# Neighbourhood attention in one fp32 encoder-layer kernel: prompt tiles of 8 columns by 16 rows with three key blocks

## What is computed

```python
r0 = jnp.clip(r - kh // 2, 0, rows - kh)      # kh = 8 (4 in the sample)
c0 = jnp.clip(c - kw // 2, 0, GRID_W - kw)    # kw = 16
bias = rpb[:, dr + (NA_KH - 1), dc + (NA_KW - 1)]
s = einsum('bqhd,bqnhd->bhqn', q_r, k_r) * scale + bias
out = einsum('bhqn,bqnhd->bqhd', softmax(s), v_r)
```

## Time and profile before

| | |
|---|---|
| median of 3 runs | 2660.97 us (2659.28 to 2661.75) |
| the profiled execution | 2659.89 us |
| its span in the trace | 2658.1 us |
| PE busy | 2525.8 us (95%) |
| DVE, ACT, POOL busy | 1561.6 us (59%), 1276.1 us (48%), 392.6 us (15%) |
| chain that ended last, by engine | PE 94%, DVE 3%, ACT 1%, issue 1% |
| of it on lines of attention | L1463 3%, L1476 2%, and part of L1325's 28% |
| granted PE clock, mean | 0.966 |

### The profile page before, as it was taken

The page is one execution under the profiler, slowest core; times in us unless marked ns, Lnnn a source line. Parts: engine busy times, 40 slices in busy tenths (PEclk is TensorE's granted clock), DMA queues, the critical chain, the costliest instruction groups (busy, mean ns, idle before and its releaser), DMA issues.

```text
span 2658.1 us, 43740 instructions
## 1 busy us (share of the span) xinstructions
PE 2525.8 (95%) x17770; PEld 2144.8 (81%) x17770; DVE 1561.6 (59%) x2106; ACT 1276.1 (48%) x1826; POOL 392.6 (15%) x221
## 2 busy tenths in 40 slices
PE   7979999999999989829999999999999999999997
PEld 4666767767777668629999999999999999999997
DVE  3343242341010133368888888887888888888885
ACT  3113243331000021217767776776677667767763
POOL 0041201011111100020220221022012202210210
PEclk9988999999999999959999999999999999999999
DMA  8111101010010133328988988898899889888972
GB/s 185 35 32 30 30 8 30 0 40 24 24 47 24 32 151 133 142 83 284 296 270 291 312 285 267 300 317 270 288 304 296 271 282 322 285 276 303 321 269 84
DMA packets 338366, 481.41 MB, mean 181 GB/s; under 512 B 22059, under 2 KB 194746, under 8 KB 338209
## 3 DMA queue, kind: packets, MB, share of 16 engines
q1 hardware_dynamic: 331072, 454.26, 50.9%
q0 software_dynamic: 7136, 24.93, 4.7%
HBM read 454.29 MB, written 24.87 MB: 180 GB/s over the span
## 4 chain that ended last, share of the span: by engine, by line
PE 94%; DVE 3%; issue 1%; ACT 1%; DMA 0%; POOL 0%; SPq 0%; DVEq 0%; ACTq 0%; POOLq 0%
PE ps L1615 35%; PE ps L1325 28%; PE ps L1618 16%; PE ps L1538 4%; PE ps L1463 3%; PE ps L1476 2%; PE ps L1605 1%; PE ps L1606 1%; PE ps L1423 1%; PE ps L1654 1%; PE ps L1655 1%; DVE top_i L1208 0%; DVE aff L1210 0%; DVE top_v L1207 0%; PE ps L1548 0%
## 5 line engine op out<-in xcount | busy, mean ns | idle before, releaser
L444 DVE TENSOR_TENSOR w_lo<-raw,w_hi 128x2048 bf16<-128x2048 f32 x380 | 868.0, 2287 | 182.1 <-ACT w_hi L864 181.7
L1615 PE MATMUL ps<-x_hl,w_hi 128*128 128x320 f32 x4096 | 728.3, 320 | 5.7 <-issue 5.7
L864 ACT ACTIVATE w_hi<-raw 128x2048 fp32r<-128x2048 f32 x384 | 731.5, 1906 | 0.1
L1615 PEld LDWEIGHTS ps<-x_hl,w_hi 128*128 128x128 f32 x4096 | 606.4, 189 | 6.2 <-issue 5.9
L1618 PE MATMUL ps<-x_b,w_lo 128*128 128x160 bf16 x4096 | 372.9, 234 | 0.0
L1615 PE MATMUL ps<-act_hl,w_hi 128*128 128x320 f32 x2048 | 350.8, 324 | 1.1 <-DVE act_hl L1271 1.1
L1615 PEld LDWEIGHTS ps<-act_hl,w_hi 128*128 128x128 f32 x2048 | 313.0, 195 | 3.2 <-DVE act_hl L1271 1.3
L1618 PEld LDWEIGHTS ps<-x_b,w_lo 128*128 128x128 bf16 x4096 | 271.3, 98 | 52.5 <-issue 0.2
L732 POOL DMA_INDIRECT y_out<-ye_p,idx_scatter x16 | 83.1, 5191 | 1110.1 <-DVE ye_s L1286 1110.1
L883 ACT ACTIVATE lows<-ps 128x320 f32<-128x320 f32 x256 | 112.0, 437 | 197.3 <-PE ps L1618 197.3
L837 ACT ACTIVATE sig<-ps 128x512 f32<-128x512 f32 (+1 forms) x48 | 25.3, 526 | 316.5 <-PE ps L1325 316.5
(11 more groups left out here) (197 smaller groups left out, 2857.9 us busy)
## 6 DMA issues: line engine op xcount, KB each, us to landing
raw<-in_w_g SPq DMA_DIRECT2D x64, 2048.0 KB, 9.3
raw<-in_w_u SPq DMA_DIRECT2D x64, 2048.0 KB, 9.7
raw<-in_w_d SPq DMA_DIRECT2D x64, 2048.0 KB, 11.2
m_raw<-in_w_in SPq DMA_DIRECT2D x16, 512.0 KB, 4.7
h_raw<-in_w_in SPq DMA_DIRECT2D x12, 512.0 KB, 4.0
x_in<-in_x SPq DMA_DIRECT2D x10, 512.0 KB, 4.3
x_res<-in_x SPq DMA_DIRECT2D x10, 512.0 KB, 4.1
y_out<-x SPq DMA_DIRECT2D x10, 512.0 KB, 2.9
```

The source lines that it names most:

```text
L444: engine.tensor_tensor(unit(w_lo, v), raw_half(v), unit(w_hi, v).bitcast(F32), ALU.subtract)\
L864: act.activation(unit(w_hi, w), raw_half(w), ACT.Copy).then_inc(hi_ready, 1)
L1615: pe.matmul(out, unit(w_hi, v)[:, k, cols], hl[:, k, :, :].rearrange("p a n -> p (a n)"), start=k == 0, stop=False)
```

## The change

The prompt's queries, keys and values are kept by columns: token number 16 × column + row. A tile of 128 queries is now 8 columns by all 16 rows. Its keys are the 8 columns themselves and their two neighbours of 8 columns, all rows: three blocks of 128, two at either edge of the grid. The sample keeps its two-row tiles with 256 keys. Of the 20 halves 12 have 384 keys and 8 have 256. Rows outside a query's window are now masked by value, too.

- Q, K and V are written into `qkvT` by columns (`by_columns`), `onaT` back by rows.
- Scores are one matmul of up to 384 columns, into four single banks in turn (4 to 7); transposes go to banks 2 and 3 in turn; there are four `p_sb` slots for three.
- Scores and bias run three halves ahead (`AHEAD`), and ACT copies j before exponent(j+3).
- All transposes of V stand behind the last product.
- The bias comes from a second DRAM tensor, `shifted_dram` (the table padded to 31 rows, 16 copies for each head). Per pair SP issues 16 loads of it, 16 partitions × 16 rows × 24 words each, and four of `skew_dram` for the sample. POOL adds a row mask to `raw_near`, read with rows and columns exchanged, adds the column mask for the sample, and cuts the window's column bounds into `bias_inner` with two selects per head. At the start POOL builds the row mask, spreads it with eight DMAs and writes `shifted_dram` ahead of `skew_dram`.

The core of the diff:

```diff
 def attention_tiles():
     tiles = []
-    for base, rows in ((0, S_PROMPT // GRID), (S_PROMPT, S_SAMPLE // GRID)):
-        kh = min(KH, rows)
-        for r in range(0, rows, 2):
-            lo = min(max(r - kh // 2, 0), rows - kh)
-            hi = min(max(r + 1 - kh // 2, 0), rows - kh) + kh
-            tiles.append((base + lo * GRID, hi - lo, lo - r + KH - 2, hi - lo > kh))
+    last = S_PROMPT // P - 1
+    for i in range(S_PROMPT // P):
+        lo, hi = max(i - 1, 0), min(i + 1, last)
+        tiles.append((lo, hi - lo + 1, "all" if i == 0 else "edge" if i == last else "inner"))
+    for r in range(0, S_SAMPLE // GRID, 2):
+        tiles.append((PT_TILES, 2, r))
     return tiles
...
+        def by_columns(n, c):
+            if c == 2:
+                return qkvT[:, n, S_PROMPT:TOK]
+            half = ROWS // 2
+            return qkvT[:, n, 0:S_PROMPT].rearrange("p (c r) -> p r c", r=ROWS)[:, half * c:half * c + half, :]
+        def as_rows(ap, c):
+            return ap if c == 2 else ap.rearrange("p (r c) -> p r c", c=GRID)
...
             def bias_loads(hp):
+                heads = shifted[bass.ds(hp * 2, 2), :, :]
+                for j in range(TILE_COLS):
+                    for hh in range(2):
+                        near = bass.AP(heads.tensor, heads.offset + hh * ROWS * PAD + (ROWS - 1) * RPB_W + TILE_COLS - 1 - j,
+                                       [[PAD - RPB_W, ROWS], [RPB_W, ROWS], [1, NEAR]])
...
+                        rows = skew[bass.ds((hp * 2 + hh) * RPB_H + (KH - S_ROWS + 1 - ri), S_BIAS), :, :]
                         src = bass.AP(rows.tensor, rows.offset + (GRID - 1),
-                                      [[SKEW - 1, GRID], [GRID * SKEW, BIAS_ROWS], [1, GRID]])
-                        sp.dma_start(bias_raw[GRID * ri:GRID * ri + GRID, hh, :, :], src).then_inc(b_loaded, 16)
+                                      [[SKEW - 1, GRID], [GRID * SKEW, S_BIAS], [1, GRID]])
+                        sp.dma_start(raw_sample[GRID * ri:GRID * ri + GRID, hh, :, :], src).then_inc(b_loaded, 16)
...
-                sp.wait_ge(b_step, hp * 8 - 6)
+                sp.wait_ge(b_step, hp * 8 - 4)
...
+            for j in range(TILE_COLS):
+                pool.dma_start(row_mask[ROWS * j:ROWS * j + ROWS, :], row_mask_1[:, :]).then_inc(mask_loaded, 16)
+            pool.dma_start(mask_sb[:, :], col_mask).then_inc(mask_loaded, 16)
+            pool.wait_ge(pad_loaded, 32)
             pool.wait_ge(f_tables, 16 * 4)
+            pool.dma_start(shifted, rpb_wide[:, :].rearrange("q (o x) -> q o x", o=1)
+                           .broadcast_to([HEADS, ROWS, PAD])).then_inc(skew_stored, 16)
             pool.dma_start(skew, rpb_pad[:, :].rearrange("q (o x) -> q o x", o=1)
                            .broadcast_to([HEADS * RPB_H, GRID, SKEW])).then_inc(skew_stored, 16)
-            pool.dma_start(mask_sb[:, :], col_mask).then_inc(mask_loaded, 16)
-            pool.wait_ge(mask_loaded, 16)
+            pool.wait_ge(mask_loaded, 16 * (TILE_COLS + 1))
...
+                    pool.tensor_tensor(bias_near[:, hh, :, :], raw_near[:, hh, :, :].rearrange("p r y -> p y r"),
+                                       rows_b, ALU.add).then_inc(b_step, 1)
+                    pool.tensor_tensor(bias_sample[:, hh, :, :], raw_sample[:, hh, :, :],
+                                       mask_b.broadcast_to([P, S_BIAS, GRID]), ALU.add).then_inc(b_step, 1)
...
+                    pool.affine_select(out=bias_inner[:, hh, :, :], in_=bias_near[:, hh, :, :], compare_op=ALU.is_ge,
+                                       fill=MASKED, base=ROWS - 1, pattern=[[ROWS, NEAR], [0, ROWS]],
+                                       channel_multiplier=-1).then_inc(b_step, 1)
+                pool.wait_ge(b_step, hp * 8 + 6)
+                apart(pool, pool_passed)
+                for hh in range(2):
+                    pool.affine_select(out=bias_inner[:, hh, :, :], in_=bias_inner[:, hh, :, :], compare_op=ALU.is_ge,
+                                       fill=MASKED, base=(KW - 1) * ROWS, pattern=[[-ROWS, NEAR], [0, ROWS]],
+                                       channel_multiplier=1).then_inc(b_step, 1)
             for n in range(3):
                 weight_parts(0, n)
...
-                        act.activation(qkvT[:, 2, c0:c0 + cn], bank(j % 3, cn), ACT.Copy).then_inc(h_vT, 1)
+                        act.activation(by_columns(2, j % 3), as_rows(bank(j % 3, cn), j % 3), ACT.Copy)\
+                           .then_inc(h_vT, 1)
...
-                    if j < 18:
-                        exponent(j + 2)
-                    nk = TILES[j // 2][1] * GRID
-                    full = min(nk // P, 4)
+                    blocks = TILES[j // 2][1]
                     act.wait_ge(p_tr, hp * 20 + (j + 1))
                     if j >= 2:
                         act.wait_ge(pv_done, hp * 20 + (j - 1))
-                    if nk > 4 * P:
-                        act.activation(pT[j % 2][0:GRID, 4, :], bank(3, P, slice(0, GRID)), ACT.Copy)
-                    act.activation(pT[j % 2][:, 0:full, :], bank(2, full * P).rearrange("p (k n) -> p k n", n=P),
+                    act.activation(pT[j % 2][:, 0:blocks, :],
+                                   bank(2 + j % 2, blocks * P).rearrange("p (k n) -> p k n", n=P),
                                    ACT.Copy).then_inc(p_copied, 1)
+                    if j + AHEAD < 20:
+                        exponent(j + AHEAD)
...
-                    dve.scalar_tensor_tensor(qkvT[:, n, c0:c0 + cn], bank(j % 3, cn), qk_g[:, n:n + 1],
-                                             rinv[j % 2][:, 0:cn], ALU.mult, ALU.mult).then_inc(h_qk, 1)
+                    dve.scalar_tensor_tensor(by_columns(n, j % 3), as_rows(bank(j % 3, cn), j % 3), qk_g[:, n:n + 1],
+                                             as_rows(rinv[j % 2][:, 0:cn], j % 3), ALU.mult, ALU.mult)\
+                       .then_inc(h_qk, 1)
...
-                        out=p_sb[u][:, 0:nk], in0=ps[:, 2048 + 1024 * b:2048 + 1024 * b + nk],
-                        in1=table.rearrange("p r c -> p (r c)"), scale=1.0, scalar=-3.0e38,
+                        out=p_sb[u][:, 0:nk], in0=bank(4 + j % 4, nk),
+                        in1=bias_of(j).rearrange("p r c -> p (r c)"), scale=1.0, scalar=-3.0e38,
...
+                    if t < PT_TILES:
+                        out = onaT[:, bass.ds(hp, 1), 0:S_PROMPT].rearrange("p o (r c) -> p (o c) r", c=GRID)\
+                            [:, TILE_COLS * t:TILE_COLS * t + TILE_COLS, :]
+                        src = bank(t % 2, P).rearrange("p (c r) -> p c r", r=ROWS)
+                    else:
+                        out = onaT[:, bass.ds(hp, 1), P * t:P * t + P]
+                        src = bank(t % 2, P).rearrange("p (o n) -> p o n", o=1)
+                    dve.tensor_scalar(out, src, 1.0, None, ALU.mult).then_inc(o_out, 1)
+                for j in range(AHEAD):
...
-                    if j >= 7:
-                        values(j - 7)
-                values(2)
+                for c in range(len(CHUNKS)):
+                    values(c)
...
+                    if j >= 4:
+                        pe.wait_ge(s_added, hp * 20 + (j - 3))
+                    pe.matmul(bank(4 + j % 4, P * blocks), qkvT[part, 0, P * t:P * t + P],
+                              qkvT[part, 1, P * first:P * (first + blocks)], start=True, stop=True).then_inc(s_ready, 1)
+                def transposed(j):
+                    pe.wait_ge(p_ready, hp * 20 + (j + 1))
                     if j >= 2:
-                        pe.wait_ge(s_added, hp * 20 + (j - 1))
-                    n = min(rows * GRID, BANK)
-                    op = pe.matmul(ps[:, at0:at0 + n], qkvT[part, 0, P * t:P * t + P],
-                                   qkvT[part, 1, key0:key0 + n], start=True, stop=True)
-                    if rows > KH:
-                        op = pe.matmul(ps[:, at0 + n:at0 + n + P], qkvT[part, 0, P * t:P * t + P],
-                                       qkvT[part, 1, key0 + n:key0 + n + P], start=True, stop=True)
-                    op.then_inc(s_ready, 1)
-                def transposed(j):
-                    nk = TILES[j // 2][1] * GRID
-                    pe.wait_ge(p_ready, hp * 20 + (j + 1))
-                    if j >= 1:
-                        pe.wait_ge(p_copied, hp * 20 + j)
-                    for k in range(min(nk // P, 4)):
-                        op = pe.transpose(bank(2, P, first=P * k), p_sb[j % P_SLOTS][:, P * k:P * k + P], ident[:, :])
-                    if nk > 4 * P:
-                        op = pe.transpose(bank(3, P, slice(0, GRID)), p_sb[j % P_SLOTS][:, 4 * P:nk], ident[:, :])
+                        pe.wait_ge(p_copied, hp * 20 + (j - 1))
+                    for k in range(TILES[j // 2][1]):
+                        op = pe.transpose(bank(2 + j % 2, P, first=P * k), p_sb[j % P_SLOTS][:, P * k:P * k + P],
+                                          ident[:, :])
...
```

(61 more changed lines are left out.)

63 lines of the change are left out of this document (32 added, 31 removed).

## The result

The changed kernel takes 2676.68 us, median of 4 runs (2675.86 to 2678.73); the kernel before took 2660.12 beside it (2656.37 to 2661.75). The ratio is 1.0065, 95% interval 1.0048 to 1.0083: **slower by 0.65%**, where 2.6% less was forecast.

A forecast was written before the change was run, and what follows sets the result against it. PE was taken to bound the attention phases. Terms of 17.0 + 0.4 + 0.8 − 0.7 = 17.5 us a pair, 70.0 for four, took 2659.9 to 2589.9; predicted 2591 us, range 2573 to 2620 for 8 times in 10.

The forecast's parts named there:

- the clock: Attention phases: 40.7 us at half clock, 20.3 us lost over four phases, taken to stay as it is.
- the rival with chance 0.03: Attention phases: the clock drops at the starting gap and does not return within the phase; 2738 us, chance 0.03.
- The price of a low us: Attention phases: each us at the low clock costs half a us.
- V's transposes: Before the first scores: four transposes move behind the last product, exposing a copy; cost 0.7 us a pair, ends 0 and 1.4.
- the tail: End of attention phase: ACT's copy comes before exponent, cutting PE's 0.94 us idle; 0.8 us less, ends 0 and 0.94.
- Sum, 17.5 a pair: All terms together: 17.5 us less per pair of heads, 70.0 us for four.
- The third block: Inner half of 384 keys: 2.08 us of PE at full clock, bounds 2.0 to 2.20.
- Can the others follow?: Attention halves: DVE at 1.52 and ACT at 1.31 us a half stay under 2.08, so PE remains the bound.
- The hand-over rival: Inner halves: hand-overs between engines bind, 2.4 to 2.66 us a half; 2606 to 2619 us, chance 0.14.
- Start: Attention start, first score to first transposes: 0.4 us less than 3.91, ends 0 and 1.5.
- Strided writes: DVE's writes of Q, K and V: 393 ns more a copy, hidden by the third product, so no cost.
- The rule that spoke against the change: Attention phases: brief PE idling makes the clock fall oftener, half-clock time doubling to 81 us; 2611 us, chance 0.12.

The follow-up runs named there:

- step: The changed kernel with one unused 128-row matmul of 384 columns ahead of the products of each half, gaps unfilled: 2624.0 us, ratio 0.9893.
- rows64: step with its added matmul on 64 rows, same columns: 2737.5 us, ratio 1.0294.
- turns: The changed kernel with two more unused transposes in each inner half, gaps unfilled: 2625.4 us, ratio 0.9862.
- late: fill with POOL's split of the gates' weights held back until eight tiles of the last pair are done: 2573.2 us, ratio 0.9682.
- before_fill: The kernel before with 10 unused 128x512 products per pair in its three idle gaps at the attention start: 2644.0 us, ratio 0.9941.
- fill: The changed kernel with 15 unused 128x512 products per pair in PE's idle gaps at the attention start: 2599.6 us, ratio 0.9777.
- hold: fill with POOL's split of the gates' weights held back until two tiles of the last pair are done: 2587.0 us, ratio 0.9725.
- scores_first: late with V's transposes and copies moved behind scores(3), into the gap, and six unused products for the fillings: 2579.2 us, ratio 0.9714.
- gap64: late with all fillings on 64 rows: 2570.9 us, ratio 0.9667.
- gap2: late without the five fillings between V's transposes, the ten ahead of the first transposes kept: 2574.2 us, ratio 0.9688.

## Why the prediction was wrong

**The step that failed** is the clock: "The gaps at the start stay, so I leave this loss as it is." The fall stayed (1.00, then 0.65, then 0.50), and the gaps in sum grew: PE idled 0.73, 1.01 and 0.64 us in the kernel before and idles 0.44, 0.61 and 2.31 now, since four scores stand ahead of the first transposes and none between. But the loss also depends on the return, and that was taken from a different steady part. What came true is the rival with chance 0.03, and the argument against it, "it ended by itself after about 10 us each time, with the same mix of matmuls", was the mistake: the 7 to 14 us were a result of the old matmuls. step, rows64 and turns show that the matmuls of the steady part set it. The rival's border, 45 us low a phase, held: the changed kernel with 57.6 to 62 is slower, step and turns with 20 and 27 on average are faster.

**The price of a low us** was put at 0.5 and measured less. The ratios of the changed kernel and late differ by 0.0383, 102 us for 239 low: 0.43 (0.40 to 0.45 with both intervals). An inner half goes from 2.12 to 3.88 us, 1.83 times and not twice. The rival put a low phase at 81 us, 74 of PE's work and 7 idle; the windows show 62.5 to 64.0 and 2.9 to 3.8, so its 2738 was far too high. In all, 102 us for the low clock, less the 16 that the kernel before lost already, less 69 gained, give 17 us more, as measured; this is the difference of the same runs split into parts, not a further test of the price.

**The other terms held in sum**, once the clock is out of the way; V's transposes and the tail were mis-sized by some 0.3 to 0.5 us each:

- *Sum, 17.5 a pair.* From the first scores of a pair to the next pair's are 306.43 − 218.25 = 88.18 us in late and 324.43 − 218.73 = 105.70 in before_fill, 17.52 less. The ratios give 0.9941 − 0.9682 = 0.0259, 69 us, for 70.0. That the sum fits to 0.02 us is partly luck. From the first transposes to the next projection, the blocks with the tail, are 346.25 − 310.14 = 36.11 us against 382.06 − 328.49 = 53.57, 17.46 less for 17.8, and what that lacks V's transposes give back.
- *The third block.* An inner half at full clock is 2.12 us for 2.08 (bounds 2.0 to 2.2).
- *Can the others follow?* Yes: in late DVE is busy 25.5 us and ACT 21.8 of 39.8, PE 38.8. The hand-over rival is out.
- *V's transposes.* From the last product to the first scores are 334.58 − 332.10 = 2.48 us against 1.81, 0.67 more. But part of this is the four moved transposes, which stood ahead of the last product before. From the start of the last eight 512-column matmuls ahead of it, a stretch that holds the same work in both kernels, to the first scores are 334.58 − 327.41 = 7.17 us against 330.28 − 323.35 = 6.93. So the move costs 0.24 us, not 0.7: the term took the whole copy as uncovered. The idle times are 0.44 and 0.61 us where one of 0.73 was. The two starts, before and with the change:

```profile
323.35 1.98 PE L1325 MATMUL ps<-hx_hi,w_low 128*128 128x512 f32 x8
...
327.41 1.98 PE L1392 MATMUL ps<-hx_hi,w_low 128*128 128x512 f32 x8
```
- *Start.* 338.25 − 334.58 = 3.67 us against 3.91: 0.24 less for 0.4. Of these 3.67 us PE idles 2.31 at a stretch, and that trips the clock.
- *Tail.* The 0.94 us idle is 0.40 in late, 0.54 less for 0.8, and none at low clock.
- *Strided writes, POOL's tables, SP's loads* cost nothing, as argued. Two views of the changed kernel, DVE's scaling into `qkvT` by form, and SP's issues, then POOL's timeline:

```profile
L1089 DVE SCALAR_TENSOR_TENSOR qkvT<-ps,qk_g,rinv 128x512 f32<-128x512 f32 x16 | 17.9, 1118 | 98.0 <-ACT rinv L844 98.0
...
L522 SPq DMA_DIRECT2D raw_near<-shifted_dram x64: 316/317/1203, 73.4 to 443.3; - x64
L529 SPq DMA_DIRECT2D raw_sample<-skew_dram x16: 598/604/672, 82.0 to 446.3; - x16
```
```profile
286.23 1.18 POOL L693 TENSOR_TENSOR bias_near<-raw_near,row_mask 128x384 f32<-128x384 f32 x1 [63.89 <-DVE onaT L1143]
...
292.25 1.30 POOL L706 TENSOR_SCALAR_AFFINE_SELECT bias_inner<-bias_inner 128x384 f32<-128x384 f32 x2 [0.22 <-POOL bias_inner L700]
...
301.53 1.04 POOL L679 CAST w_high<-h_raw 128x1024 fp32r<-128x1024 f32 x1 [7.98 <-PE ps L1392]
```

The scaling takes 1118 ns (forecast 0.75 + 0.39 = 1.14), and PE waits for it nowhere. POOL's tables take 293.55 − 286.23 = 7.3 us (forecast 7.2 to 9.0) and leave 7.98 idle. An issue of the near table takes 317 ns, not the 985 taken from the old form, so 64 + 16 issues cost SP 30 us in all.

**The rule that spoke against the change.** By the Trainium skill (TensorE: Matmul & The Clock Gate, "A second HAM failure mode: psum-queue depth-cycling") short idle times between groups make the clock oscillate. I gave it 0.12 and 2611. Its direction was right, since idle time trips the clock; its picture was not, since the trace shows one fall a phase, no return, and no idle time in the low stretch.

**What stays open.** In the steady part at hand, the 128-row work (transposes and products) has about the same share of a half before and after: (0.69 + 1.38) / 3.35 = 62%, with the fifth block's product counted in, which has 64 rows, and (3.88 − 1.57) / 3.88 = 60%. The kernel before still returned after about 10 us and the changed one doesn't. The runs show that more 128-row work tips it and wider scores don't, but not which property of the old sequence was enough. Nor is it known how much idle time trips it. Single ones of 1.16 us (fill) and 1.57 us (hold) came before a fall, ones of 1.15 us (scores_first) and 1.10 us (late, ahead of the gates' first product) did not in the profiled executions. The length of one is not the whole of it: the kernel before fell in all four phases behind two or three idle times of 0.64 to 1.02 us close together, none of them longer. Its first phase, PE timeline and a window of 1 us:

```profile
219.42 1.13 PE L1463 MATMUL ps<-qkvT 64*128 64x512 f32 x4 [0.73 <-DVE v_tok L1042]
221.57 1.71 PE L1463 MATMUL ps<-qkvT 64*128 64x512 f32 x2 [1.02 <-DVE row_max L1056]
...
222.00:223.00 1.00, 1.00 (x2) 0.00 (x0) 0.93 (x5) 0.83 (x3) 0.00 (x0) 0.50 0.06 20
```

## What to carry to other kernels

Where a granted clock is under 1.00 in a stretch that the change touches, price the fall and the return apart: ask which idle time starts the low stretch and which work ends it, and whether the change alters that work; a recovery seen in the old code is no promise for the new. A change that takes matmuls away can lose all of its gain there (70 us here), and a few useless matmuls in the idle gap ahead of it, with POOL's work held back as well, get it back: late and gap64 take 2573 and 2571 us, 3.2 to 3.3% less than the kernel before. Of that 0.6% is to be had in the kernel before too (before_fill). Keep the work of other engines that delays PE's feeder, here POOL's subtraction beside DVE's normalisation, away from such a stretch, too.

## What the runs showed of the hardware

- The low clock can last through PE busy 4.00 of 4.00 us, for 57 us and more, in a sequence of matmuls that holds the full clock when nothing has tripped it (late, 1.00).
- Matmuls on 64 rows fill an idle gap as well as those on 128 (gap64, 1.00), but added to the steady part they didn't restore the clock (rows64, 317 us low); matmuls on 128 rows and transposes did (step 82 us, turns 109).
- Idle times of 0.73 and 1.02 us within 3 us were followed by a fall (first phase of the kernel before), ones of 0.44 and 0.61 us were not (gap2).
- A us at half clock cost 0.43 us, not 0.5, for these small matmuls of 128 to 384 columns.
- DVE's scaling by a column, SBUF to SBUF, grew from some 0.4 to 1.67 and 2.55 us beside POOL's subtraction of 1,024 columns, and PE's gap behind it (1.16 and 1.57 us) was enough for the clock to fall.
